# Weights laid out slab by slab, one contiguous run per partition, for a diffusion layer with 16 experts on one core

## The reference

```python
cap = EC_FACTOR * (B * T) // N_EXPERTS          # 128 latent rows, 16 context rows per expert
aff = jax.nn.softmax((xt @ router_w).astype(jnp.float32), axis=-1)
gate_vals, idx = lax.top_k(aff.T, cap)
xe = xt[idx]
hid = jax.nn.silu(jnp.einsum('ecd,edf->ecf', xe, w1)) * jnp.einsum('ecd,edf->ecf', xe, w3)
ye = jnp.einsum('ecf,efd->ecd', hid, w2) * gate_vals[..., None]
y = jnp.zeros_like(xt).at[idx.reshape(-1)].add(ye.reshape(-1, D).astype(xt.dtype))
```

## Time and profile before

| | |
|---|---|
| median of the runs | 1633.41 us (lowest 1632.48) |
| the profiled execution: own time, span | 1631.1 us, 1629.3 us |
| PE, DVE, ACT, POOL busy | 97%, 44%, 24%, 29% |
| mean granted TensorE clock | 0.992 |
| moved by DMA | 324.85 MB, mean 199 GB/s |
| expert stage, about 850 to 1616 us | PE busy nearly throughout, about 300 GB/s |

### The profile page before, as it was taken

The page is one execution under the profiler, slowest core; times in us unless marked ns, Lnnn a source line. Parts: engine busy times, 40 slices in busy tenths (PEclk is TensorE's granted clock), DMA queues, the critical chain, the costliest instruction groups (busy, mean ns, idle before and its releaser), DMA issues. The chain is left out here.

```text
span 1629.3 us, 28403 instructions
## 1 busy us (share of the span) xinstructions
PE 1580.3 (97%) x11180; PEld 1377.1 (85%) x11180; DVE 716.6 (44%) x1871; ACT 387.4 (24%) x970; POOL 477.5 (29%) x560
## 2 busy tenths in 40 slices
PE   6999999999999899999988999999999999999997
PEld 5866876666668767788878999999999999999997
DVE  4001046776565844222364244444334454433344
ACT  5210113341221466411131111111111111111114
POOL 3000000015232643121203343433344343334432
PEclk9999999999999999999999999999999999999999
DMA  9302212132202486423269899999899999999985
GB/s 346 114 11 85 82 39 59 36 125 30 59 29 93 133 239 204 157 66 103 91 212 353 290 299 297 316 322 298 278 293 304 291 315 329 299 286 285 315 263 228
DMA packets 225582, 324.85 MB, mean 199 GB/s; under 512 B 36015, under 2 KB 116008, under 8 KB 225466
## 3 DMA queue, kind: packets, MB, share of 16 engines
q1 hardware_dynamic: 185817, 282.70, 51.7%
q0 software_dynamic: 15568, 17.45, 5.7%
q10 hardware_dynamic: 24080, 23.02, 4.8%
HBM read 294.42 MB, written 25.51 MB: 196 GB/s over the span
## 5 line engine op out<-in xcount | busy, mean ns | idle before, releaser
L1973 PE MATMUL psum<-arena 128*128 128x144 f32 x4096 | 504.5, 286 | 1.7 <-DVE arena L2615 1.7
L1973 PEld LDWEIGHTS psum<-arena 128*128 128x128 f32 x4096 | 502.8, 190 | 1.9 <-ACT arena L1350 1.9
L1985 PE MATMUL psum<-arena 128*128 128x144 f32 x2048 | 257.3, 288 | 6.3 <-ACT arena L1391 5.0
L1985 PEld LDWEIGHTS psum<-arena 128*128 128x128 f32 x2048 | 254.8, 192 | 7.1 <-ACT arena L1391 5.2
L1556 PE MATMUL psum<-arena 128*128 128x384 f32 x720 | 242.9, 493 | 0.0
L889 POOL DMA_INDIRECT expert_list<-gt x128 | 129.8, 1014 | 317.2 <-DVE gt L2645 287.6
L1556 PEld LDWEIGHTS psum<-arena 128*128 128x128 f32 x720 | 134.5, 191 | 90.0 <-issue 2.9
L2675 DVE TENSOR_TENSOR arena<-gt,psum 128x144 f32<-128x144 f32 x128 | 38.8, 303 | 360.8 <-PE psum L1973 359.8
L2497 DVE SCALAR_TENSOR_TENSOR arena<-arena,gt 128x1024 f32<-128x1024 f32 x128 | 159.1, 1280 | 0.5 <-DMA arena<-affinity_rows 0.5
L1559 PE MATMUL psum<-arena 128*128 128x256 f32 (+2 forms) x784 | 146.4, 346 | 0.0
L1559 PEld LDWEIGHTS psum<-arena 128*128 128x128 f32 x784 | 129.4, 190 | 15.5 <-issue 1.7
(11 more groups left out here) (379 smaller groups left out, 1629.4 us busy)
## 6 DMA issues: line engine op xcount, KB each, us to landing
arena<-in_exp_w SPq DMA_DIRECT2D x96, 2048.0 KB, 11.8
arena<-in_ada_w SPq DMA_DIRECT2D x24, 1024.0 KB, 7.0
arena<-in_w_in SPq DMA_DIRECT2D x11, 1024.0 KB, 5.2
arena<-in_x_sample SPq DMA_DIRECT2D x16, 512.0 KB, 4.8
arena<-affinity_rows SPq DMA_DIRECT2D x16, 512.0 KB
arena<-m_decay_rows ACTq DMA_DIRECT2D x36, 128.0 KB, 3.2
arena<-decay_rows ACTq DMA_DIRECT2D x24, 192.0 KB, 3.4
out<-arena SPq DMA_DIRECT2D x9, 512.0 KB, 2.6
```

Of the source, the lines that this page charges most:

```text
L1973: ins = mm(bank[:, 0:SLOTS], w[:, k, col], xeT[:, k, :], start=(k == 0), stop=(k == KD - 1))
L1985: ins = mm(bk[4 + db % 2][:, 0:SLOTS], wslot[4 + db // 4][:, k, (db % 4) * P:(db % 4) * P + P], hid[:, k, :], start=(k == 0), stop=(k == K ...
```

## The change

Each slab is stored in DRAM in the order in which SBUF holds it, so that what a partition gets is one run: 16 KB for the experts' slabs, 8 KB for those of ada_w, w_out and the wide ones of w_in. The host writes the arrays so; the loads take the slab as partitions x elements. The destination, the order of the DMAs, their semaphores and their waits are as before, and so is which row of the matrix lies in which partition and k-block.

```diff
+def slab_starts(slabs):
+    starts, used = {}, 0
+    for s, slab in enumerate(slabs):
+        if slab is not None and slab[0] == "win":
+            starts[s] = used
+            used += D * slab[2]
+    return starts
...
-    w_in_v = w_in.rearrange("(k p) n -> p k n", p=P)
-    ada_v = ada_w.rearrange("(k p) n -> p k n", p=P)
-    wout_v = w_out.rearrange("(k p) n -> p k n", p=P)
-    w_src = {"ada": ada_v, "win": w_in_v, "wout": wout_v}
+    in_first = slab_starts(slabs)
+
+    def slab_source(s):
+        mat, a, n = slabs[s]
+        if mat == "win":
+            return w_in[in_first[s]:in_first[s] + D * n].rearrange("(p k n) -> p k n", p=P, n=n)
+        return {"ada": ada_w, "wout": w_out}[mat][a // SLAB].rearrange("p (k n) -> p k n", n=n)
...
-                sp.dma_start(ring[:, s % RING, :, 0:n], w_src[mat][:, :, a:a + n]).then_inc(slab_in[s % RING], 16)
+                sp.dma_start(ring[:, s % RING, :, 0:n], slab_source(s)).then_inc(slab_in[s % RING], 16)
...
-            w13 = [w.rearrange("e (p k) f -> e p k f", p=P) for w in (exp_w1, exp_w3)]
-            w2v = exp_w2.rearrange("e (k p) d -> e p k d", p=P)
             def expert_slab(e, q):
-                half_q, src = (q // 2, w13[q % 2]) if q < 4 else (q - 4, w2v)
-                one = src[e:e + 1] if isinstance(e, int) else src[bass.ds(e, 1)]
-                one = one.rearrange("e p k f -> (e p) k f")
-                sp.dma_start(wslot[q], one[:, :, 512 * half_q:512 * half_q + 512]).then_inc(w_in_slot[q], 16)
+                src = (exp_w1, exp_w3)[q % 2][e, q // 2] if q < 4 else exp_w2[e, q - 4]
+                sp.dma_start(wslot[q], src.rearrange("p (k f) -> p k f", k=KD)).then_inc(w_in_slot[q], 16)
...
+    def column_slabs(w, n):
+        return w.reshape(KD, P, -1, n).transpose(2, 1, 0, 3).reshape(-1, P, KD * n)
...
-        ... ("ada_w", ada_w[0][:, ada_order]), ("w_in", w_cols), ... ("w_out", w_out[0]),
-        ("exp_w1", exp_w1[0]), ("exp_w3", exp_w3[0]), ("exp_w2", exp_w2[0][:, :, order]), ...
+        ... ("ada_w", column_slabs(ada_w[0][:, ada_order], SLAB)), ("w_in", w_tiles), ...
+        ("w_out", column_slabs(w_out[0], SLAB)), ("exp_w1", _np.stack([column_slabs(w[order], 512) for w in exp_w1[0]])),
+        ("exp_w3", ...the same of exp_w3...), ("exp_w2", _np.stack([column_slabs(w[:, order], 512) for w in exp_w2[0]])), ...
```

More of the change, by code:

```diff
@@ L534, in load_slab @@
                     return
-                mat, a, n = slabs[s]
+                n = slabs[s][2]
                 read = [t for t in range(s % RING, s, RING) if t in last_read]
@@ L2759 @@
     rpb[192:-192] = rows
+    def column_slabs(w, n):
+        return w.reshape(KD, P, -1, n).transpose(2, 1, 0, 3).reshape(-1, P, KD * n)
+    w_tiles = _np.concatenate([column_slabs(w_cols[:, a:a + n], n).reshape(-1)
+                               for m, a, n in (x for x in plan_slabs() if x is not None) if m == "win"])
     order = _np.arange(D).reshape(P, KD).T.reshape(-1)
@@ L2769 @@
         ("state_sT", state_ssm[0, 0].reshape(2, GS, RS, HD, HD).transpose(0, 1, 4, 2, 3).reshape(2, P, RS * HD)),
-        ("vec_rows", vec_rows), ("small_row", small_row), ("ada_w", ada_w[0][:, ada_order]), ("w_in", w_cols), ("rpb_pad", rpb),
-        ("w_out", w_out[0]), ("router_w", router_w[0]), ("exp_w1", exp_w1[0]), ("exp_w3", exp_w3[0]),
-        ("exp_w2", exp_w2[0][:, :, order]), ("final_g", final_g),
+        ("vec_rows", vec_rows), ("small_row", small_row), ("ada_w", column_slabs(ada_w[0][:, ada_order], SLAB)), ("w_in", w_tiles), ("rpb_pad", rpb),
+        ("w_out", column_slabs(w_out[0], SLAB)), ("router_w", router_w[0]), ("exp_w1", _np.stack([column_slabs(w[order], 512) for w in exp_w1[0]])), ("exp_w3", _np.stack([column_slabs(w[order], 512) for w in exp_w3[0]])),
+        ("exp_w2", _np.stack([column_slabs(w[:, order], 512) for w in exp_w2[0]])), ("final_g", final_g),
     ]
```

## The result

The changed kernel is slower: 1676.03 us (1655.04 to 1690.18) against 1632.95, ratio 1.022 with an interval of 1.019 to 1.025, so that it is slower, but not surely by over 2%. The times of this document are medians of all executions, while ratios and intervals leave out those in a slower state (here 1690.18, and 5169.05 of the kernel before). The forecast was 1632.5 us, within 1626 to 1647. The profiled execution took 1655.04 us, span 1653.3, and is the lowest of the four: the trace lacks some 20 us of what the median has, and whether these are more of the same loss it can't show.

A forecast was written before the change was run, and what follows sets the result against it. PE, busy in 97% of the span, was taken as the bound. Terms -0.7 + 0 + 0 + 0 on the profiled 1631.1 us gave 1630.4; the median lying 2.3 higher gave 1632.7, written as 1632.5, range 1626 to 1647.

The forecast's parts named there:

- Expert slabs, steady experts: 0 us: Weight loads from the third expert on: faster landing gains nothing, having 18 us to spare; 0, ends -0.2 and +0.5 us an expert.
- PE has no gap: Claim that from the third expert on each repeats after 47.04 us with PE never idle in it.
- the slower rival: List's scatters to first expert's gathers: small transfers wait behind 16 KB runs; +15 or +5 us, 1637 to 1648; chance 0.18.
- the +5 to +15: First expert's gathers queued behind 16 KB runs: +15 us alternating run for run, +5 if four rows go in one turn.
- a slack of 0.4 us: Steady experts: about 0.4 us between DVE finishing the gathered rows and PE starting the second products.
- 0.7 us forecast: Ada and w_in slabs at the start: four slabs carried faster, -0.7 us, bounds 0 and 1.09, passed on to the end.
- my faster rival: Start: with less idle PE's clock may stay up, worth 1.7 us, up to -5 in all (1628); chance 0.14.
- the second slower rival: All experts: transfer rate falls through the new partition distance; at 300 GB/s +20 us, 1652; chance 0.05.
- the two slower cases: Small transfers waiting behind long runs (1637 to 1650, chance 0.18) and a lower transfer rate (1650 to 1680, chance 0.05).

## Why the prediction was wrong

**The step that failed** is "Expert slabs, steady experts: 0 us". It said that even a gather that waited for all weights ahead of it would be in by about 1121, no later than now. It let the gathers issue when they do in the earlier trace rows and asked only how long they wait then. But POOL issues them only when its scatter-adds have landed, and the last of those is issued just before slab 0 (1107.76 in the earlier trace rows). Timeline of POOL before:

```profile
1105.99 1.55 POOL L938 DMA_INDIRECT moe_latent<-arena,gt  x1 [0.30 <-issue]
```

It ends at 1107.54. Where an engine isn't through with its rows when the weights come, each row left waits for a run, and the gathers start 5 to 8 us later. In two experts of the trace they then meet the second pair, which I had counted as coming after them. The list of waits had it all along: POOL's wait for moe_latent, 55.3 us in 12 pieces, the longest 7.9, was in the trace before and is not in the prediction. Nor is PE's wait of 1.21 us in expert 6: "PE has no gap" holds for the experts of the earlier trace rows, but expert 6 took 48.64 us, so the chain had run over its slack once already.

**The price of a turn was right, its place and one count were not.** I gave 0.64 us a run and charged it to the first expert alone, as the slower rival. There PE's wait grew by 3.65 us, less than the +5 to +15 I wrote. The +15 counted 4 gathers x 8 rows = 32 turns; the traces, that of before too, record a gather as 32 packets of 4 KB, two for each engine, which makes 8 turns for the four. In the steady experts, where I gave +0.5 us each as the upper end, the trace has +22.6 us in eight of them. I took it that nothing lands later than the weights ahead of it, and read no loss from that, with a slack of 0.4 us and a chain of two small transfers in a row.

**The start gained by another way than the forecast's.** 0.7 us forecast, 2.6 measured. The slabs do come faster, with 423 GB/s in the window of 18 to 21, more than the 412 that I took as the best row, and PE's wait of 1.09 us for the fourth slab is gone. But it was not passed on: PE now waits 1.17 us for ACT where it waited 0.22, and the next products start at 28.22 instead of 28.41. What is gained is the clock. It stayed at 1.00 (2.4 GHz) from 24 to 33, where the earlier trace rows have 0.75 and 0.68, with 0.50 (1.2 GHz) from 28.6 to 31.8; so eight matmuls take 1.97 us instead of 3.65, and the next ada product starts 1.9 us ahead (30.45, was 32.33). PE had been busy for 1.90 of the 3 us from 24 to 27, and not for 1.06. That was my faster rival, worth 1.7 us, at a chance of 0.14; that the forecast's sign came out is luck. The last 0.7 us up to expert 0 I have not followed. Windows of the kernel after:

```profile
18.00:21.00 3.00, 2.66 (x31) 1.69 (x29) 2.33 (x4) 2.50 (x6) 1.45 (x5) 1.00 1.00 423
...
24.00:27.00 3.00, 1.90 (x23) 1.05 (x21) 1.72 (x6) 1.42 (x4) 0.27 (x5) 1.00 1.02 429
27.00:30.00 3.00, 1.83 (x12) 1.63 (x9) 0.43 (x1) 1.34 (x2) 0.00 (x0) 1.00 1.02 421
30.00:33.00 3.00, 3.00 (x28) 2.22 (x27) 0.16 (x1) 0.38 (x1) 0.00 (x0) 1.00 0.72 265
```

**The rate did not fall**, as forecast, and the second slower rival has nothing for it: a slab lands sooner. Its own threshold was reckoned wrong, too: by its terms a loss of 33 us needs 282 GB/s, not 260.

**On the rule of the Trainium skill** ("DMA: Bandwidth & Descriptors", Queues, rings and completion order) that an engine drains some 9 to 17 descriptors before it turns to another queue: the trace does not agree for these runs. Rows 0.70, 0.40, 0.25 and 0.18 us apart leave room for one run of 16, 8, 4 or 2 KB between them and not for nine. The series 6.72, 7.60, 8.70, 11.55 us alone would not have told the two apart. Another sentence of the page, in SWDGE vs HWDGE vs iDMA, gives a packet as at most 4096 B preferably; runs of 2 and 4 KB are within it and cost nothing here, 16 KB are not; but 8 KB are not either, and took 1633.30 us, no longer than the kernel before. I had read the first and weighed it against the first expert only.

**The chances.** I had 0.23 on the two slower cases and 0.05 beyond 2%. The mechanism that came had 0.18, but with a price that ended at 1650. The sign that I gave for it, a wait of 10 us or more in the first expert, didn't come (8.61); the sign for being wrong, a steady expert over 47.1 us, did.

## What to carry to other kernels

Longer DMA runs made the bulk transfers of this kernel faster and the small transfers beside them slower: one of these waits about one run for each packet that it has left on an engine, and one late engine is enough. Before lengthening runs, list the small transfers that stand in a chain with little slack and see which bulk transfer is issued in the same microseconds, not only for the last link but for each that feeds it. If bulk has room, make it wait for the small ones, and look then what is queued behind it. Here 16 or 8 KB runs with that one wait gave 0.5% (1625.4 and 1625.6 us against 1633.5 and 1633.7), of which the start's new layout has 0.2 by itself, and the same wait with 2 KB runs cost up to 2.3%.

## What was not expected of the hardware

- With the same order and distance of the two issues (0.12 to 0.22 us) the wait is 3.5 to 4.2 us in five experts and 8.65 to 9.80 in six. I take the number of long waits for what spreads the changed kernel's times (35 us between lowest and highest). One more trace speaks for it: an execution of 1713.09 us, of the kernel with the experts alone in the new layout, has 11 of 12 waits of 8.5 us or longer, and PE waits 51.1 us for DVE at its second products in ten pieces, against 17.4 in six here. It was not shown on several executions of one kernel.
- After a long wait of PE the clock is low: in expert 6 the 114 matmuls behind the 10 us wait take 16.43 us where 114 x 122.5 ns are 14.0, so 2.4 us come on top of the 10. The 0.86 below is a mean of both levels: 0.50 (1.2 GHz) from 1185 to 1190, 1.00 (2.4 GHz) after. The wait of 1.21 us before, in the same place, has no such cost: 114 matmuls in 14.36 us behind it. The granted clock of the wait and of the stretch behind it, in the kernel after (columns: stretch, its length, busy us of PE, PEld, DVE, ACT and POOL, clock, DMA share, GB/s):

```profile
1173.50:1185.40 11.90, 1.93 (x16) 1.72 (x15) 2.34 (x6) 0.12 (x1) 1.15 (x2) 0.76 0.88 366
1185.40:1202.00 16.60, 16.52 (x117) 16.52 (x117) 12.97 (x33) 3.54 (x12) 4.24 (x5) 0.86 0.36 128
```

- DVE shows 39.7 us of waits at L2684 that the trace puts down to "remote", up to 7.1 us, in the changed kernel. The kernel with only the start changed has 39.1 us of them and loses nothing by it. What they are stays open.
